# A hybrid layer on one core: forgetting scores as two passes of split operands in a new tile order, and a rebuilt output projection of the mixer

## What is computed

```python
def forgetting_attention(q, k, v, log_f):            # 8 heads, width 64
    qf = q * (dh ** -0.5)
    c = jnp.cumsum(log_f, axis=1).transpose(0, 2, 1)
    for i in range(S // Q_BLOCK):                     # 8 blocks of 128 queries
        L = (i + 1) * Q_BLOCK                         # keys up to the diagonal
        s = einsum('bhqd,bhkd->bhqk', qf[:, :, q0:L], kf[:, :, :L])
        s = s + c[:, :, q0:L, None] - c[:, :, None, :L]
        p = softmax(where(mask, s, -inf)); out = p @ v[:L]

o = concat([head_rms_norm(o_fox), head_rms_norm(o_gla) * silu(gate)])   # 512 + 512
y = o @ w_out                                         # 1024 x 1024
```

## Time and profile before

| | |
|---|---|
| median of 3 runs | 2369.24 us |
| the profiled execution's own time | 2369.01 us |
| its span, first to last instruction | 2367.2 us |
| PE busy | 2267.3 us (96%), 10640 matmul records |
| DVE busy | 1097.8 us (46%) |
| ACT busy | 773.0 us (33%) |
| POOL busy | 468.8 us (20%) |

### The profile page before, as it was taken

One profiled execution on the slowest core, in us unless ns is written; L12 is line 12 of the kernel. 1 busy time (PEld: TensorE's weight loads), 2 busy tenths in 40 slices (PEclk: granted clock), 3 DMA queues, 4 the chain that ended last, 5 costly groups with the idle time before them and its releaser, 6 DMA issues. The chain is left out here.

```text
span 2367.2 us, 27049 instructions
## 1 busy us (share of the span) xinstructions
PE 2267.3 (96%) x10640; PEld 1846.8 (78%) x10640; DVE 1097.8 (46%) x1356; ACT 773.0 (33%) x1210; POOL 468.8 (20%) x447
## 2 busy tenths in 40 slices
PE   5999999999999999999999899999699999999997
PEld 4788888888878777878777687778588888887886
DVE  7544444464455444452344443244844444454446
ACT  6433333331223522331222243343533333332113
POOL 2343444300021000000321100001443444410003
PEclk8999999999999999999988999999899999999999
DMA  3222222253333000011121152032122222243323
GB/s 116 89 89 72 89 72 89 93 174 94 112 108 90 20 10 19 19 31 59 63 81 54 45 178 89 18 107 89 54 89 71 89 72 90 72 143 125 113 83 125
DMA packets 105823, 194.94 MB, mean 82 GB/s; under 512 B 8113, under 2 KB 73666, under 8 KB 102882
## 3 DMA queue, kind: packets, MB, share of 16 engines
q1 hardware_dynamic: 105698, 193.21, 25.2%
HBM read 153.28 MB, written 39.91 MB: 82 GB/s over the span
## 5 line engine op out<-in xcount | busy, mean ns | idle before, releaser
L1330 PE MATMUL ps<-xc,wg 128*128 128x512 f32 x1232 | 484.3, 393 | 28.7 <-DVE xc L1853 23.3
L1331 PE MATMUL ps<-xc,wg 128*128 128x512 f32 x1232 | 482.6, 392 | 0.0
L1332 PE MATMUL ps<-xc,wg 128*128 128x512 f32 x1232 | 482.3, 391 | 0.0
L1330 PEld LDWEIGHTS ps<-xc,wg 128*128 128x128 f32 x1232 | 233.6, 190 | 80.2 <-issue 22.0
L1348 PE MATMUL ps<-d_w,d_hid 128*128 128x512 f32 x704 | 275.2, 391 | 2.9 <-DVE d_w L1885 2.8
L1349 PE MATMUL ps<-d_w,d_hid 128*128 128x512 f32 x704 | 274.5, 390 | 0.0
L1350 PE MATMUL ps<-d_w,d_hid 128*128 128x512 f32 x704 | 274.5, 390 | 0.0
L1331 PEld LDWEIGHTS ps<-xc,wg 128*128 128x128 f32 x1232 | 233.7, 190 | 48.5
L1332 PEld LDWEIGHTS ps<-xc,wg 128*128 128x128 f32 x1232 | 233.3, 189 | 48.8
L1859 DVE TENSOR_TENSOR wg<-w_sums,wg 128x1024 fp32r<-128x1024 f32 x88 | 124.7, 1418 | 188.7 <-ACT wg L831 188.7
L1895 DVE TENSOR_TENSOR y<-y,ps 128x1024 f32<-128x1024 f32 x88 | 107.4, 1221 | 216.3 <-PE ps L1350 216.3
(11 more groups left out here) (271 smaller groups left out, 3817.3 us busy)
## 6 DMA issues: line engine op xcount, KB each, us to landing
w_raw<-in_w_ff_gate SPq DMA_DIRECT2D x22, 1024.0 KB, 6.7
w_raw<-in_w_ff_up SPq DMA_DIRECT2D x22, 1024.0 KB, 5.3
hid_dram<-hid SPq DMA_DIRECT2D x22, 1024.0 KB, 4.6
raw<-hid_dram SPq DMA_DIRECT2D x44, 512.0 KB, 3.8
raw<-in_w_ff_down SPq DMA_DIRECT2D x44, 512.0 KB, 3.7
raw<-in_w_mix_in SPq DMA_DIRECT2D x24, 512.0 KB, 3.9
x_row<-x_dram SPq DMA_DIRECT2D x24, 512.0 KB, 4.2
x_dram<-x_ring SPq DMA_DIRECT2D x16, 512.0 KB, 5.0
```

Of the source, the lines that this page charges most:

```text
L1330: mm(acc, hi, x_hi, start=STARTS[q] and k == 0, stop=False, skip_group_check=True)
L1331: mm(acc, hi, x_lo, start=False, stop=False, skip_group_check=True)
L1332: last = mm(acc, lo, x_hi, start=False, stop=k == 3, skip_group_check=True)
```

## The change

It touches the mixer alone, in these parts.

1. **Scores.** q_head and k_head become four fp32r operands. `qa` holds the high part of q twice, `ka` the high and the low part of k, on 128 rows; `qb` and `kb` hold the low part of q and the high part of k, and 4 rows for c in two parts and constants, on 68 rows. One tile of scores is `qa`·`ka` and then `qb`·`kb`, each one fp32r matmul for up to 512 columns; narrower ones are widened to 256 columns. `keep_q` has three ACT copies for each half (one before), three DVE instructions for a half of q (one before) and two for a half of k (one before), and `keep_k1` one more copy for a half of k. `c` is split in two parts instead of negated.
2. **Order.** `FOX_ORDER` lists the 16 tiles of a pair: the four short tiles of head 0 from wide to narrow, then the two heads in turn.
3. **Keys.** The second half of the pair's keys is projected in pieces around scores(0) and behind the first transposes. `keep_q` of that half stands inside the tile loop, on ACT at a = 2 and 3, on DVE at a = 4. For the first pair a part of that projection now stands behind `gate_sums(1)`.
4. **Weights.** Two buffers for split weights instead of three; the split of S_GQ + 2 moves behind the last pair, and PE's `turn_k(0)` moves behind the product that uses it.
5. **Output projection.** Both halves of a tile are turned through bank 3; the forgetting half has two buffers. `gla_first` no longer waits for `o_t_lo`. `turn_o(i + 1, 0)` stands ahead of `out_tile(i)`; behind it come `turn_o(i + 1, 1)` and then both `gla_out`. DVE runs `low_o(i + 1, 1)` ahead of `scale_y(2, i)`; ACT runs `high_o(i + 1, 1)` ahead of `square1(2, i)`. The last tile is multiplied into banks 0 and 1, without waiting for `scale_y` of the tile before.

```diff
+FOX_ORDER = ((0, 3), (0, 2), (0, 1), (0, 0), (1, 0), (1, 1), (0, 4), (1, 2), (0, 5), (1, 3), (0, 6), (1, 4),
+             (0, 7), (1, 5), (1, 7), (1, 6))
...
             def scores(p, a):
-                hh, b = divmod(a, 8)
+                hh, b = FOX_ORDER[a]
+                if a in (0, FOX_LONG[0]):
+                    pe.wait_ge(proj_dve, event(S_Q + 2 * p + 1, 1 if a else 0))
+                if a == FOX_FIRST[hh]:
+                    pe.wait_ge(c_in[hh], 32 * p + 32)
+                if a in (FOX_FIRST[1], FOX_LONG[1]):
+                    pe.wait_ge(kb1_done, 2 * p + (2 if a == FOX_LONG[1] else 1))
...
-                    mm(acc[:, 0:w], q, k_head[hh][0:66, t * HT:t * HT + w], start=True, stop=not diagonal)
+                    cols = slice(t * HT, t * HT + max(w, 2 * P))
+                    mm(acc[:, 0:max(w, 2 * P)], qa[hh][:, tile_of(b)], ka[hh][:, cols], start=True, stop=False)
+                    mm(acc[:, 0:max(w, 2 * P)], qb[hh][:, tile_of(b)], kb[hh][:, cols], start=False, stop=not diagonal)
...
             def attend_fox(p):
+                late, bank = S_Q + 2 * p + 1, 3 if p else 1
+                project(late, 1, bank, 0 if p else 6, 14 if p else 18)
                 scores(p, 0)
+                project(late, 1, bank, 14 if p else 18, 19 if p else 21)
...
+                    if a == 1:
+                        project(late, 1, bank, 19 if p else 21)
...
-                for t in range(2):
+                for t in range(1 if p + 1 < PAIRS else 2):
                     project(S_Q + 2 * p + 3, t, 2 + t)
...
             def turn_o(i, b):
                 if b:
                     pe.wait_ge(o_normed, i + 1)
-                    pe.wait_ge(att_kept, min(i + 2, NT))
...
-                wait(pe, o_t_lo, 2 * i - 1 + b)
+                wait(pe, o_t_lo, 2 * i + b)
...
-                    last = nc.tensor.transpose(ps[:, 3 - 3 * b, tile_of(k)], src[:, tile_of(k)], ident[:, :])
+                    last = nc.tensor.transpose(ps[:, 3, tile_of(k)], src[:, tile_of(k)], ident[:, :])
...
-            project(S_Q + 1, 1, 1)
+            project(S_Q + 1, 1, 1, 0, 6)
             pe.wait_ge(e_suf_done, 2)
             gate_sums(1)
...
             for i in range(NT):
                 if i + 2 < NT:
                     gla_first(i + 2)
                 pe.wait_ge(o_t_lo, 2 * i + 2)
-                pe.wait_ge(d_lo_done, S_0 + S_MQ)
-                out_tile(2, i, o_t, lambda a, k, h: (h_hi, h_lo)[a][:, 4 * h:4 * h + 4, tile_of(k)])
                 if i + 1 < NT:
                     turn_o(i + 1, 0)
-                if i + 2 < NT:
-                    gla_out(i + 2, 0)
+                pe.wait_ge(d_lo_done, S_0 + S_MQ)
+                out_tile(2, i, lambda k: [t[:, k % 4, :] for t in turned_half(i, k // 4)],
+                         lambda a, k, h: (h_hi, h_lo)[a][:, 4 * h:4 * h + 4, tile_of(k)])
                 if i + 1 < NT:
                     turn_o(i + 1, 1)
                 if i + 2 < NT:
-                    gla_out(i + 2, 1)
+                    for s in range(2):
+                        gla_out(i + 2, s)
```

The same on DVE:

```diff
             def attend_fox(p):
                 splits = {6: S_Q + 2 + 2 * p, 8: S_Q + 3 + 2 * p}
...
+                    if a == 4:
+                        keep_q(S_Q + 2 * p + 1, 1, 2 if p else 0)
+                    if a == 7:
+                        keep_k1(p, 1)
...
             dve.wait_ge(c_made, NT)
-            ve.tensor_scalar(c_sb[1][:, :], c_sb[0][:, :], -1.0, None, ALU.mult).then_inc(c_done, 1)
-            keep_q(S_Q + 1, 1, 0)
+            ve.tensor_copy(c_part[0][:, :], c_sb[:, :]).then_inc(c_split, 1)
+            dve.wait_ge(c_split, 1)
+            ve.tensor_tensor(c_part[1][:, :], c_sb[:, :], f32(c_part[0][:, :]), ALU.subtract).then_inc(c_done, 1)
...
                 if i + 1 < NT:
                     norm_g(i + 1)
-                    low_o(i + 1, 0)
+                    low_o(i + 1, 1)
                 scale_y(2, i)
-                if i + 1 < NT:
-                    low_o(i + 1, 1)
```

More of the change, by code:

```diff
@@ L34 @@
 PAIRS = FOX_H // 2
+FOX_ORDER = ((0, 3), (0, 2), (0, 1), (0, 0), (1, 0), (1, 1), (0, 4), (1, 2), (0, 5), (1, 3), (0, 6), (1, 4),
+             (0, 7), (1, 5), (1, 7), (1, 6))
+FOX_WIDE = tuple(sum(b >= 4 for _, b in FOX_ORDER[:a]) for a in range(17))
+FOX_FIRST = tuple(min(a for a, (h, _) in enumerate(FOX_ORDER) if h == i) for i in range(2))
+FOX_LAST = tuple(max(a for a, (h, _) in enumerate(FOX_ORDER) if h == i) for i in range(2))
+FOX_LONG = tuple(min(a for a, (h, b) in enumerate(FOX_ORDER) if h == i and b >= 4) for i in range(2))
 MEM_H = 4
@@ L564, in _ @@
                 if p + 1 < PAIRS:
-                    sp.wait_ge(score_done, 16 * p + 16)
-                    load_c(p + 1)
+                    for i in range(2):
+                        sp.wait_ge(score_done, 16 * p + FOX_LAST[i] + 1)
+                        load_c(p + 1, i)
             for k in range(KT):
@@ L984, in keep_q @@
                         act.wait_ge(x_sent[i], 16)
-                dst, factor = ((q_head, FOX_D ** -0.5), (k_head, 1.0))[(n - S_Q) % 2]
-                sc.activation(dst[0][0:FOX_D, half(t)], ps[0:FOX_D, bank + t, :], ACT.Copy,
-                              scale=factor).then_inc(proj_act, 1)
+                c = half(t)
+                if (n - S_Q) % 2 == 0:
+                    parts = ((qa[0], 0, 0), (qa[0], FOX_D, 0), (qa[1], FOX_D, FOX_D))
+                else:
+                    parts = ((ka[0], 0, 0), (kb[0], 0, 0), (ka[1], FOX_D, FOX_D))
+                for dst, to, at in (parts[i] for i in which):
+                    op = sc.activation(dst[to:to + FOX_D, c], ps[at:at + FOX_D, bank + t, :], ACT.Copy,
+                                       scale=1.0 if (n - S_Q) % 2 else FOX_D ** -0.5)
+                if 2 in which:
+                    op.then_inc(proj_act, 1)
             def gate_logs(g, i, what):
@@ L1073, in high_o @@
                 act.wait_ge(o_turned, 2 * i + b + 1)
[L1074 to L1075 removed]
+                wait(act, rows_done, i if b else i - 1)
+                sc.activation(turned_half(i, b)[0][:, :, :], cols4(ps[:, 3, :]), ACT.Copy).then_inc(o_t_hi, 1)
             def keep_mq(c, t, bank):
@@ L1385, in value_tile, with project @@
                           lambda k: [fvw[a][k // 4][:, k % 4, :] for a in range(2)]).then_inc(v_done, 1)
-            def project(n, t, bank):
+            def project(n, t, bank, m0=0, m1=3 * KT):
                 pe.wait_ge(d_lo_done, S_0 + n + 1)
                 w = wr_of(n)
-                for k in range(KT):
-                    last = three(ps[:, bank, :], [w[a][:, k, :] for a in range(2)], [h[:, k, half(t)] for h in (h_hi, h_lo)],
-                                 k == 0, k == KT - 1)
-                last.then_inc(proj_done, 1)
+                for m in range(m0, m1):
+                    i, part = divmod(m, 3)
+                    last = mm(ps[:, bank, :], w[part // 2][:, i, :], (h_hi, h_lo)[part % 2][:, i, half(t)], start=m == 0,
+                              stop=m == 3 * KT - 1, skip_group_check=True)
+                if m1 == 3 * KT:
+                    last.then_inc(proj_done, 1)
             def gates(g):
@@ L1572, in out_tile @@
                             pe.wait_ge(d_lo_done, S_0 + S_MO + k + 1)
-                        last = three(ps[:, out_bank(bd, i) + h, :], [t[:, k, :] for t in o], [w(a, k, h) for a in range(2)],
+                        last = three(ps[:, out_bank(bd, i) + h, :], o(k), [w(a, k, h) for a in range(2)],
                                      k == 0, k == KT - 1)
@@ L1730, in _ @@
                     gla_out(0, i - 2)
-                if i == 5:
-                    for b in range(2):
-                        turn_o(0, b)
+                if i in (4, 5):
+                    turn_o(0, i - 4)
                 if i in (5, 6):
@@ L1767, in _ @@
                 pe.wait_ge(mo_lo, i + 1)
-                out_tile(3, i, mo_t[i % 2], lambda a, k, h: mo_w[a][:, k, half(h)])
+                out_tile(3, i, lambda k: [t[:, k, :] for t in mo_t[i % 2]], lambda a, k, h: mo_w[a][:, k, half(h)])
                 if i > 0:
@@ L2246, in _ @@
                     sum_g(0)
-                if i == 5:
-                    for b in range(2):
-                        low_o(0, b)
+                if i in (4, 5):
+                    low_o(0, i - 4)
             norm_f(NT - 1)
```

193 lines of the change are left out of this document (106 added, 87 removed).

## The result

The changed kernel took 2336.56 us (median of 4 runs, 2334.85 to 2339.64) against 2368.43 for the kernel before in the same runs (4 runs, 2367.17 to 2369.28): a ratio of 0.9869, 95% interval 0.9857 to 0.9881. The forecast was 2332.5, the range 2313 to 2350. The profiled execution took 2339.64 us, its span is 2337.9, against 2369.01 and 2367.2 before: 29.3 us of span to account for. It is the slowest of the four, 3.1 us above their median.

What follows compares the result with a forecast made beforehand. PE's own work was taken to bound the pairs of heads; waits and a lowered clock cost the output projection time. The terms summed to -36.5 us from 2369.0, giving 2332.5 us, range 2313 to 2350.

Steps and rivals of the forecast that it cites:

- scores: Attention scores: two fp32r passes replace float32, 4.42 us a head against 7.97, so -28.4 us over eight heads.
- waits in the tile loop: Attention tile loop: less PE work uncovers the chain behind short tiles, 4.9 us of waits a pair against 1.3; +14.4 us.
- start of the first pair: Ahead of the first pair's scores: more key copies delay gate sums and c, two waits of PE; +3.0 us.
- clock in the attention: Attention: two or three new waits make the clock fall, 1.2 to 1.7 us each; +3.5 us, bounds 0 and +14.
- behind the last pair: Behind the last pair: `turn_k(0)` moves behind a product of 11 us, so its wait goes; -1.4 us.
- output projection: Output projection: PE's cover outlasts the chains, -31.0 us from waits and 1.2 GHz phases, 3.4 given back; -27.6 us.
- rival 4: Attention: clock falls at the a = 6 wait and stays down through the tile loop; slower, about 2425 us; chance 0.03.
- rival 3: Output projection: row norm's chain outgrows the cover, 1.5 us of wait for each of seven tiles; 2351 us; chance 0.08.
- Rival 1: Attention loop: ACT and DVE keep up, waits stay at 1.3 us a pair, clock up everywhere; 2311 us; chance 0.17.
- Rival 2: Attention loop: bound by the chain, no gain, waits of 6.5 us a pair, 9 us of clock; 2345 us; chance 0.18.
- Rival 5: Scores: widened and 68-row fp32r matmuls cost like float32, so scores double, +64 us; 2425 us; chance 0.01.
- Its own signs: Right: output projection at 135 to 142 us, clock above 0.95, pair about 61 us; wrong: pair below 58 or above 64.

Runs made afterwards that it cites:

- fill: Changed kernel plus 13 useless fp32r matmuls of 512 columns in each pair, ahead of the transposes of tiles 3, 6 and 8: 2325.88 us, 0.9826.
- keys_whole: Changed kernel with the keys' second half projected in one piece ahead of the pair and copied ahead of its loop: 2359.44 us, 0.9974.
- late_parts: Changed kernel with weight splits behind wide tiles, DVE's two second-half key instructions apart, gate sums ahead of its first-half key instructions: 2342.61 us, 0.9904.
- last_bank: Changed kernel, but the last output projection tile writes to banks 4 and 5 again and waits for `scale_y`: 2339.2 us, 0.988.
- experiment 1: The change's halves apart, against the kernel before: output projection alone 2338.21 us, 0.9877; attention alone 2366.41 us, 1.0002.
- experiment 6: Four kernels, each the changed one with parts of the new output projection taken back; with turns and copies ordered as before: 2369.25 us, 0.9995.
- splits_late: Changed kernel with the splits of the next weights moved from short to wide tiles on ACT and DVE: 2331.19 us, 0.9846.

## Why the prediction came out right, point by point

The time was 4.1 us over the forecast, inside the range. The terms of the sum, as forecast and as the one profiled execution of the changed kernel has them:

| term | forecast | measured |
|---|---|---|
| scores | -28.4 | -24.5 |
| other work of the pairs | 0 | +1.5 |
| waits in the tile loop | +14.4 | +9.4 |
| start of the first pair | +3.0 | +1.3 |
| clock in the attention | +3.5 | about +15.5 |
| behind the last pair | -1.4 | -1.4 |
| output projection | -27.6 | -32.5 |
| sum | -36.5 | -30.7 (span: -29.3) |

- **Scores.** In a pair 16.35 us of PE before, 10.22 after (third pair): 6.1 saved, 7.1 forecast. The prices of 512, 384 and 256 columns were right; that the first pass of a tile is dearer was missing, some 0.09 us in each of 16 tiles, 1.4 in a pair.
- **Waits in the loop.** 3.7 us in a clean pair against 1.3: +2.4, forecast +3.6. The two places named with the most, a = 6 (1.9 forecast) and a = 8 (1.0), have 1.53 and 0.84. That at a = 3 has 1.1, more than forecast, from DVE's copies of the keys; those put down to ACT at a = 3 and 4 did not come.
- **Start.** Two waits, of 1.5 us behind `keep_q` and 1.0 for the DMA of c, against 1.5 and 2.0. Scores(0) started at 813.74, not 814.2, though all before it came 1.0 us later in this execution.
- **Clock in the attention.** This is the term that was mis-sized. I had two or three phases that cost 1.2 to 1.7 us each, 3.5 in all, bounds 0 and +14. The profiled execution has one phase of 6.8 us and one of 37.5, the second worth 15 us by itself (76.46 against 61.45): 15.5, outside the bounds. The medians say less, 10.7 us (changed kernel to fill), three times the term. That the falls come behind the new waits was right; the place was not a = 6, as rival 4 had it, but a = 3 (at a = 6 it fell once in keys_whole and once in late_parts). The 37.5 us are the mechanism of rival 4 ("the clock falls ... and stays down through the rest of the tile loop") in one pair of one execution; I gave it 0.03, for all four pairs. What I put against it was that a pair at 2.4 GHz had the same small matmuls before. Before, they came with blocks of up to 1.77 us of float32 scores and without waits of over 1 us; that this made the difference is likely but not shown.
- **Output projection.** No wait of `gla_first`; 0.54 ahead of the last tile (0.65 forecast), 0.53 ahead of the first. The stage was forecast at 136.6, plus 3.4 for two phases; it took 135.1 with none, which was luck in part, since half of the executions with this projection have a phase of 3.4 to 6.8 us. Of what the stage lost before, 15.5 us were waits beyond the 1.07 that stay, and the other 17 are put down to the clock. The cover of 7.5 us against the chain of 4.5 was right: tile 2 starts 18.5 us behind tile 1 (1222.8, 1241.3), 7.4 more than the 11.06 of a tile, and in last_bank the chain shows as a wait of 3.2 behind 1.35 of cover. That also rules out rival 3.
- **Rivals.** Rival 1 (2311) would have needed waits of 1.3 us a pair and no phase: the clean pairs have 3.7. Rival 2 said that the attention gains nothing, by waits of 6.5 us a pair and 9 us of clock, at 2345: its outcome is true (experiment 1: 1.0002), its waits are not. Rival 5 is out by the rows of the 896-column tile, 0.90 us for what took 1.56 as float32.
- **Its own signs.** Right were the stretch of the output projection, its clock, the two waits at the start and the place of the longest wait. But a pair above 64 us was named as a sign that it is wrong, and the second pair has 76.46 (65.0 to 65.1 in four of the five other executions). A clean pair has 3.7 us of waits, just below the 4 to 6 named, and the longest is 1.53 and not near 2.

The sum of the measured terms misses the span by 1.4 us, and that is two misses that cancel. The output projection started 4.4 us later than before (1201.91 against 1197.54), where the terms ahead of it give 1.8; 1.0 of the rest came ahead of the mixer, 1.6 is not accounted for. And what stands behind that stage took 1.2 us less. So the time was right partly since errors cancel: 12 us too little for the clock in the attention and 4 too much for the scores, against 5 too much for waits and 5 too little gained in the output projection. With the 10.7 us of the medians for the clock, the attention's terms and the one behind the last pair come to -3.0, near the 1.7 us by which the changed kernel lies below the output projection alone.

What stays open: why the same wait of 1.1 us is followed by a fall in one pair and not in the next. The second and the third pair have the same instructions; one has a phase in five of six executions, of 13.7 or 37.5 us, and the other never. Open too is whether the useless matmuls help by ending waits or by their dense work.

## What to carry to other kernels

Price a removed wait at its length plus half of the phases at 1.2 GHz that stand behind it: in the output projection the two were of one size (14.3 and 15.4 us in experiment 6). Take less than half where PE waits inside the phase anyway: in the attention's second pair a phase of 13.7 us cost 3.6, since the waits at a = 6 and 8, 1.5 and 0.8 us, shrank to 0.2 in all. And where heavy matmuls are replaced by fewer light ones, look for waits near 1 us among what is left, before counting the saving: here such waits took back 9.4 and the clock 10.7 to 15.5 of the 24.5 us saved. If the waits can't be removed, five or so dense matmuls into a free bank at those places are a cheap trial: 1.2 us a pair gave 23.5 us back here, 12.1 against `splits_late`. Profile more than one execution before a phase is priced: the same attention code showed phases of 13.7 to 44.4 us in all.

## What the runs showed of the hardware that was not expected

- Useless work made a kernel faster, twice, with intervals that don't touch: 0.9869 to 0.9826 and 0.9904 to 0.9801.
- Once at 1.2 GHz, a loop of transposes and 64-column matmuls stayed there for 37.5 us in one execution (13.7 us in four others, at the same place), with PE busy 74.94 of 76.46 us of that pair; in the output projection, with tiles of 11 us of 512-column matmuls, phases ended after 3.4 to 10.2 us.
- The clock fell without a wait: in five of ten executions, some 4 to 6 us behind the first tile of the output projection, among transposes and 128-column matmuls, with no wait over 0.53 us in the stage before it.
- The first matmul of 512 columns behind a run of 64-column ones takes 0.32 us to the next start, the others 0.23.
